# The first k-tile behind three post-norms split into an old-X part and a normalised part

## Chip, cores and metric

One core of one Trainium2 chip. The metric is the device time of the whole kernel in microseconds (us), the median of several runs; lower is better.

## What is computed

Two transformer blocks over a sequence of 512 with model width 1024, all in f32. The first has a mixer (convolution and eight-head forgetting attention), a memory cross attention and a squared-ReLU MLP; each of these three is wrapped in an RMS norm before and an RMS norm behind:

```python
for l in range(DEPTH):
    h = rms_norm(x, norm_mix_pre[l])
    y = hybrid_mixer(h, ...)
    x = x + rms_norm(y, norm_mix_post[l])
    h = rms_norm(x, norm_mem_pre[l])
    y = memory_cross_attention(h, mem_n, ...)
    x = x + rms_norm(y, norm_mem_post[l])
    h = rms_norm(x, norm_mlp_pre[l])
    y = squared_relu_mlp(h, w_up[l], w_down[l])
    x = x + rms_norm(y, norm_mlp_post[l])
```

The second block (differential attention with a pooling mixer, an MLP, gated linear attention, an MLP) has only norms ahead. The change touches the three places where `x = x + rms_norm(y, post)` is followed by a norm and a projection of the new x: into the memory queries, into the MLP and into the second block's queries.

## The kernel before

Everything is transposed: a tensor of width 1024 is eight tiles of 128 partitions by 512 tokens, so `X[:, t, :]` is tile t of the residual stream. Every weight matrix comes as 292 units of 128 x 1024 f32 values, which SyncE loads in a fixed order into four slots of `RAW`. GpSimd splits each unit into a high part `WH` (rounded to fp32r, line 278) and a low part `WL` (the rest, line 283) as soon as the unit that held the slot is used up (semaphore `unit_done`). An activation is split too, into `AH` (ScalarE) and `AL` (VectorE), and each product is three matmuls: WH x AH, WH x AL, WL x AH. The order on each engine is the order of the code; semaphores join the engines.

A projection that follows a norm starts with a **quad** (`quad`, lines 387 to 419): four output tiles in PSUM banks 0 to 3 are built together, one k-tile (one input tile) after the other, 12 matmuls of 128x512 each, so that TensorE can start as soon as the first input tile is there. A norm's row scale is applied to the output (`RB`), so the quad works on x times the gain, not on the normalised x.

In front of three of these quads stands a **post-norm**:

- `y_out` (ScalarE, lines 1327 to 1335) squares each tile of y and stores y times its gain in `Y`; VectorE sums the squares in `y_sum`; TensorE forms the column sum in bank 7 with two products by a matrix of ones (`post_stat`, lines 451 to 455), and ScalarE makes 1/sqrt of it in bank 7 (lines 1105 and 1107). After the MLP the same is done with `post=True`.
- `x_update` (VectorE, lines 1898 to 1920): for each tile, `scaled(t)` writes Y x bank 7 into a bank (line 1903), the next instruction adds that to X (line 1913), and `low` makes `AL` from X and `AH` (line 1593). `add_square` adds the squares of the new x (line 1907), for the next norm's statistic.
- `normed_post` (ScalarE): for each tile of the new X the high part `AH` (line 1120) and the square (line 1123).

In the quad behind it k-tile 0 runs its eight products with `AH` first (lines 398 and 399) and then four with `AL` (line 402); k-tiles 1 to 7 wait for `AL` (lines 413 to 415). The three post-norms are called o1 (its quad m2, the memory queries), o2 (quad m3, the MLP's first four tiles) and m3 (quad b, the second block's queries).

## Time and profile before

| | us |
|---|---|
| runs | 1835.21, 1834.85, 1832.19 |
| median of the runs | 1834.85 |
| the profiled execution, first to last instruction (span) | 1833.2 |
| TensorE busy in it | 1778.5 (97%) |
| VectorE busy | 1039.9 (57%) |
| GpSimd busy | 1055.2 (58%) |
| ScalarE busy | 452.9 (25%) |

The profile gives for the profiled execution its span alone; what lies around the span is not in it. A timeline row has the start in us, the duration, the engine, the line of the code, the operation, what it writes and reads, and in square brackets how long the engine had been idle and who ended that. PE is TensorE, PEld its weight load, DVE is VectorE, ACT ScalarE, POOL GpSimd. A matmul of 128x512 is shown with 0.39 us, but the next one starts 0.23 us after it, since they overlap; starts are the thing to compare.

### The profile page before, as it was taken

What the parts mean: (1) busy time and instruction counts of PE and PEld (TensorE: products, weight loads), DVE (VectorE), ACT (ScalarE), POOL (GpSimd) and SP (SyncE); (2) the same over time, 40 slices, a digit from 0 to 9 for tenths busy, and PEclk for the clock granted to TensorE, in tenths of its full rate; (3) what the DMA queues carried; (4) which work ended last, traced back from release to release, by engine and by line L of the source; (5) the groups of instructions that cost most, each with busy time, mean ns of one, the idle gap of its engine ahead of it and who ended that gap; (6) DMA issues with size and microseconds to landing.
All of it is one profiled execution on the core that took longest, in us unless ns stands there. A gap on an engine that the chain in (4) does not pass through costs nothing.

```text
span 1833.2 us, 22531 instructions
## 1 busy us (share of the span) xinstructions
PE 1778.5 (97%) x8318; PEld 1444.7 (79%) x8318; DVE 1039.9 (57%) x1209; ACT 452.9 (25%) x915; POOL 1055.2 (58%) x590
## 2 busy tenths in 40 slices
PE   8998899999999998999999999999999999999998
PEld 7875677788888886767888888887888888888886
DVE  4989546754343576175635252696766562626177
ACT  5215435411010123153201010212345320102011
POOL 7562462566666665533666666675344566666672
PEclk9999999999999999999999999999999999999999
DMA  6231121233333232311332333322122233333331
GB/s 238 81 97 42 47 91 47 80 92 102 94 94 101 92 102 93 92 47 47 93 102 92 104 92 98 97 92 82 56 70 60 78 98 98 93 103 92 101 94 46
DMA packets 46589, 161.42 MB, mean 88 GB/s; under 512 B 5232, under 2 KB 7792, under 8 KB 46384
## 3 DMA queue, kind: packets, MB, share of 16 engines
q1 hardware_dynamic: 45088, 157.31, 27.9%
q10 hardware_dynamic: 1424, 3.01, 0.5%
q8 instruction: 57, 0.93, 0.2%
q14 instruction: 20, 0.16, 0.0%
HBM read 158.20 MB, written 2.10 MB: 87 GB/s over the span
## 4 chain that ended last, share of the span: by engine, by line
PE 91%; DVE 6%; ACT 2%; issue 1%; DMA 0%; POOL 0%; DVEq 0%; ACTq 0%
PE bank L365 21%; PE bank L366 21%; PE bank L367 21%; PE bank L413 3%; PE bank L414 3%; PE bank L415 3%; DVE bank L1698 2%; PE bank L984 1%; PE bank L954 1%; PE bank L956 1%; PE bank L955 1%; PE bank L999 1%; PE bank L1001 1%; PE bank L1000 1%; PE bank L491 1%
## 5 line engine op out<-in xcount | busy, mean ns | idle before, releaser
L283 POOL TENSOR_TENSOR WL<-RAW,WH 128x1024 fp32r<-128x1024 f32 x291 | 739.3, 2541 | 24.3
L278 POOL TENSOR_SCALAR WH<-RAW 128x1024 fp32r<-128x1024 f32 x291 | 312.5, 1074 | 720.8 <-PE bank L367 380.0
L365 PE MATMUL bank<-AH,WH 128*128 128x512 f32 x848 | 332.2, 392 | 0.0
L367 PE MATMUL bank<-AH,WL 128*128 128x512 f32 x848 | 330.0, 389 | 0.0
L366 PE MATMUL bank<-AL,WH 128*128 128x512 f32 x848 | 330.0, 389 | 0.0
L365 PE MATMUL bank<-HH,WH 128*128 128x512 f32 x832 | 325.2, 391 | 0.0
L367 PE MATMUL bank<-HH,WL 128*128 128x512 f32 x832 | 323.9, 389 | 0.0
L366 PE MATMUL bank<-HL,WH 128*128 128x512 f32 x832 | 323.7, 389 | 0.0
L1357 ACT ACTIVATE TMP<-bank 128x512 f32<-128x512 f32 x96 | 57.2, 596 | 776.9 <-PE bank L367 739.1
L1970 DVE TENSOR_TENSOR HL<-TMP,HH 128x512 fp32r<-128x512 f32 x96 | 238.6, 2486 | 4.0 <-ACT HH L1362 0.8
L1976 DVE TENSOR_TENSOR Y<-Y,bank 128x512 f32<-128x512 f32 x72 | 49.5, 688 | 309.2 <-PE bank L367 309.2
L1966 DVE TENSOR_TENSOR TMP<-TMP 128x512 f32<-128x512 f32 x96 | 112.7, 1174 | 175.2 <-ACT TMP L1357 175.2
L365 PEld LDWEIGHTS bank<-AH,WH 128*128 128x128 f32 x848 | 159.2, 188 | 34.9 <-issue 2.0
L366 PEld LDWEIGHTS bank<-AL,WH 128*128 128x128 f32 x848 | 159.2, 188 | 34.0 <-issue 1.2
L367 PEld LDWEIGHTS bank<-AH,WL 128*128 128x128 f32 x848 | 159.2, 188 | 33.2
L365 PEld LDWEIGHTS bank<-HH,WH 128*128 128x128 f32 x832 | 156.2, 188 | 35.7 <-DVE HL L1970 3.6
L367 PEld LDWEIGHTS bank<-HH,WL 128*128 128x128 f32 x832 | 156.2, 188 | 32.7
L366 PEld LDWEIGHTS bank<-HL,WH 128*128 128x128 f32 x832 | 156.2, 188 | 32.1
L413 PE MATMUL bank<-AH,WH 128*128 128x512 f32 x208 | 81.6, 392 | 0.0
L414 PE MATMUL bank<-AL,WH 128*128 128x512 f32 x208 | 81.0, 389 | 0.0
L415 PE MATMUL bank<-AH,WL 128*128 128x512 f32 x208 | 80.9, 389 | 0.0
L1698 DVE SCALAR_TENSOR_TENSOR bank<-Y,VC,bank 128x512 f32<-128x512 f32 x116 | 78.7, 754 | 0.1
(382 smaller groups left out, 2349.4 us busy)
## 6 DMA issues: line engine op xcount, KB each, us to landing
RAW<-wstream SPq DMA_DIRECT2D x291, 512.0 KB, 3.5
out<-Y SPq DMA_DIRECT2D x8, 256.0 KB, 2.3
X<-xT SPq DMA_DIRECT2D x3, 512.0 KB, 8.1
TMP<-memT ACTq DMA_DIRECT2D x1, 1024.0 KB, 8.3
MIX<-bands ACTq DMA_DIRECT2D x1, 768.0 KB, 4.9
RAW<-wstream SPq DMA_DIRECT2D x2, 256.0 KB, 3.8
X<-xT SPq DMA_DIRECT2D x2, 256.0 KB, 4.4
BF<-masks ACTq DMA_DIRECT2D x1, 352.0 KB, 4.0
```

Source lines behind the costliest of these rows:

```text
L278: nc.gpsimd.tensor_scalar(WH[:, s, :, :].rearrange("p k n -> p (k n)"), RAW[:, s, :], 1.0, 1.0, ALU.mult, ALU.mult).then_inc(sem("w_high"), 1)
L283: nc.gpsimd.tensor_tensor(WL[:, s, :, :].rearrange("p k n -> p (k n)"), RAW[:, s, :], f32(WH[:, s, :, :].rearrange("p k n -> p (k n)")), A ...
L365: mm(bank, WH[:, slot, k, :], h(k), start=(k == 0), stop=False)
L366: mm(bank, WH[:, slot, k, :], l(k), start=False, stop=False)
L367: last = mm(bank, WL[:, slot, k, :], h(k), start=False, stop=(k == KT - 1))
L413: mm(banks[j][:], wh, h(k), start=(k == 0), stop=False)
L414: mm(banks[j][:], wh, l(k), start=False, stop=False)
L415: last = mm(banks[j][:], wl, h(k), start=False, stop=(k == KT - 1))
L1357: nc.scalar.activation(TMP[:, j % 4, :], B[banks[j] if first else j % 4][:], ACT.Relu).then_inc(sem(f"{p}_relu"), 1)
L1698: ins = v.scalar_tensor_tensor(out=SG[:, cc, :] if j == CONV_W - 1 else acc, in0=U[:, cc, j:j + S], scalar=w, in1=acc, op0=ALU.mult, op1=A ...
L1966: v.tensor_tensor(TMP[:, 4 + j % 2, :], TMP[:, j % 4, :], TMP[:, j % 4, :], ALU.mult).then_inc(sem(f"{p}_hsq"), 1)
L1970: v.tensor_tensor(HL[:, j, :], TMP[:, 4 + j % 2, :], f32(HH[:, j, :]), ALU.subtract).then_inc(sem(f"{p}_hlow"), 1)
```

## The change

The first k-tile of the quad is x_new = x_old + norm(y). The old x is there before the statistic, so its product is taken first, as a product of its own:

- `x_high` (ScalarE) and `x_low` (VectorE) split old `X[:, 0, :]` times the gain into `AH[:, 7, :]` and `AL[:, 7, :]`, places that tile 7 takes over later. They stand ahead of `y_out` and `y_sum`, and for the MLP ahead of the last down projection's read-outs.
- On TensorE `post_stat` and `quad` become `post_quad`: 12 matmuls of the old x (`x_part`, lines 470 to 472) stand behind the second ones-product (behind m3 half of them stand ahead of it), then the high products of k-tiles 0 and 1 (16), then their low products (8), then k-tiles 2 to 7 as before. `unit_done` for the first unit is signalled after k-tile 1's low products.
- VectorE rounds the normalised part itself: line 1990 writes Y x gain x bank 7 into `AH[:, 0, :]`, line 1997 the same without gain into `TMP`, and line 1999 the low part of their difference. The tiles are updated in the order 1, 2, 0, 3, ..., 7.
- In the update's loop `add_square` moves from ahead of `scaled` and `low` to behind them.
- In m3 and b later products read tile 0 of the full x as well, so ScalarE and VectorE make its high and low part once more at the end (`low(q, 0, gain)`), and the first unit behind the quad takes k-tile 0 last (`first_tile_last`).

The diff's core; the calls of `x_high`, `x_low` and `post_quad` in the places named above are left out:

```diff
+POST_ORDER = (1, 2, 0, 3, 4, 5, 6, 7)
...
+            def post_quad(p, q, n, done, bank_free=None, ahead=0, last_k=None):
+                def x_part(j):
+                    if bank_free:
+                        pe.wait_ge(sem(f"{p}_yg"), nth(f"{p}_yg", bank_free[j]))
+                    wh, wl = weights(0, j)
+                    mm(B[j][:], wh, AH[:, 7, :], start=True, stop=False)
+                    mm(B[j][:], wl, AH[:, 7, :], start=False, stop=False)
+                    return mm(B[j][:], wh, AL[:, 7, :], start=False, stop=False)
+
                 pe.wait_ge(sem(f"{p}_ysum"), nth(f"{p}_ysum", 7))
                 mm(B[7][:], ONES[:], SUM, start=True, stop=False)
+                pe.wait_ge(sem("raw_split0"), nth("raw_split0", n // 4 + 1))
+                pe.wait_ge(sem(f"{q}_xh"), nth(f"{q}_xh", 1))
+                pe.wait_ge(sem(f"{q}_xl"), nth(f"{q}_xl", 1))
+                for j in range(ahead):
+                    x_part(j)
                 pe.wait_ge(sem(f"{p}_ysq"), nth(f"{p}_ysq", 8))
                 mm(B[7][:], ONES[:], TMP[:, 5, :], start=False, stop=True).then_inc(sem(f"{p}_ystat"), 1)
+                for j in range(ahead, 4):
+                    last = x_part(j)
+                last.then_inc(sem(f"{q}_xpart"), 1)
+                for k in range(2):
+                    if k == 0:
+                        pe.wait_ge(sem(f"{q}_yh"), nth(f"{q}_yh", 1))
+                    else:
+                        pe.wait_ge(sem(f"{q}_ah"), nth(f"{q}_ah", 1))
+                    for j in range(4):
+                        wh, wl = weights(k, j)
+                        mm(B[j][:], wh, AH[:, k, :], start=False, stop=False)
+                        mm(B[j][:], wl, AH[:, k, :], start=False, stop=False)
+                for k in range(2):
+                    pe.wait_ge(sem(f"{q}_al"), nth(f"{q}_al", k + 1))
+                    for j in range(4):
+                        wh, wl = weights(k, j)
+                        last = mm(B[j][:], wh, AL[:, k, :], start=False, stop=False)
+                last.then_inc(sem("unit_done"), 1)
+                for k in range(2, KT):
+                    u = k // 2
+                    if k % 2 == 0:
+                        pe.wait_ge(sem(f"raw_split{u}"), nth(f"raw_split{u}", n // 4 + 1))
+                    pe.wait_ge(sem(f"{q}_al"), nth(f"{q}_al", k + 1))
+                    for j in range(4):
+                        if last_k and k == KT - 1 and j == 2:
+                            last_k()
+                        wh, wl = weights(k, j)
+                        mm(B[j][:], wh, AH[:, k, :], start=False, stop=False)
+                        mm(B[j][:], wh, AL[:, k, :], start=False, stop=False)
+                        last = mm(B[j][:], wl, AH[:, k, :], start=False, stop=(k == KT - 1))
+                        if k == KT - 1 and j < 3:
+                            last.then_inc(sem(done), 1)
+                    if k % 2 == 1:
+                        last.then_inc(sem("unit_done"), 1)
...
+                for n, t in enumerate(POST_ORDER):
+                    x_ready(n)
+                    if t == KT - 1:
+                        act.wait_ge(sem(f"{p}_xpart"), nth(f"{p}_xpart", 1))
+                    if t:
+                        nc.scalar.activation(AH[:, t, :], X[:, t, :], ACT.Copy, scale=vec(gain, t)).then_inc(sem(f"{p}_ah"), 1)
+                    if n >= 3:
+                        act.wait_ge(sem(f"{p}_sum"), nth(f"{p}_sum", n - 2))
+                    nc.scalar.activation(B[POST_SQ[p][n % 2]][:] if n else SUM, X[:, t, :], ACT.Square).then_inc(sem(f"{p}_xsq"), 1)
+                if p != "m2":
+                    act.wait_ge(sem("unit_done"), nth("unit_done", U0[{"m3": "mlp", "b": "bq"}[p]] + 1))
+                    nc.scalar.activation(AH[:, 0, :], X[:, 0, :], ACT.Copy, scale=vec(gain, 0)).then_inc(sem(f"{p}_ah"), 1)
+
+            def x_high(q, gain):
+                nc.scalar.activation(AH[:, 7, :], X[:, 0, :], ACT.Copy, scale=vec(gain, 0)).then_inc(sem(f"{q}_xh"), 1)
...
+                first = TMP[:, 0, :]
                 dve.wait_ge(sem(f"{p}y_rb"), nth(f"{p}y_rb", 1))
-                n = scaled(0)
-                for t in range(KT):
+                done(v.scalar_tensor_tensor(out=AH[:, 0, :], in0=Y[:, 0, :], scalar=vec(gain, 0), in1=B[7][:],
+                                            op0=ALU.mult, op1=ALU.mult).then_inc(sem(f"{q}_yh"), 1), f"{q}_yh")
+                n = scaled(POST_ORDER[0])
+                for i, t in enumerate(POST_ORDER):
                     dve.wait_ge(sem("dve_step"), nth("dve_step", n))
-                    done(v.tensor_tensor(X[:, t, :], X[:, t, :], o, ALU.add).then_inc(sem(f"{p}_x"), 1), f"{p}_x")
-                    if t >= 2:
-                        add_square(t - 1)
-                    if t < KT - 1:
-                        dve.wait_ge(sem(f"{p}_x"), nth(f"{p}_x", t + 1))
-                        n = scaled(t + 1)
-                    low(q, t, gain)
+                    done(v.tensor_tensor(X[:, t, :], X[:, t, :], o if t else first, ALU.add).then_inc(sem(f"{p}_x"), 1), f"{p}_x")
+                    if i == 0:
+                        own(v.tensor_tensor(first, Y[:, 0, :], B[7][:], ALU.mult).then_inc(sem("dve_step"), 1), "dve_step")
+                        dve.wait_ge(sem(f"{q}_yh"), nth(f"{q}_yh", 1))
+                        done(v.scalar_tensor_tensor(out=AL[:, 0, :], in0=first, scalar=vec(gain, 0), in1=f32(AH[:, 0, :]),
+                                                    op0=ALU.mult, op1=ALU.subtract).then_inc(sem(f"{q}_al"), 1), f"{q}_al")
+                    dve.wait_ge(sem(f"{p}_x"), nth(f"{p}_x", i + 1))
+                    if i < KT - 1 and POST_ORDER[i + 1]:
+                        n = scaled(POST_ORDER[i + 1])
+                    if t:
+                        low(q, t, gain)
+                    if i >= 2:
+                        add_square(i - 1)
                 add_square(KT - 1)
-
+                if q != "m2":
+                    low(q, 0, gain)
```

How the instructions stand. First VectorE at the start of the update of o1 (in the rows bank7 holds 1/sqrt, bank4 is the scratch bank of `scaled`; L1593 and L1672 are `low`). Before:

```order
L1903 TENSOR_TENSOR bank4<-Y,bank7 128x512 [waits rb,ysum]
L1913 TENSOR_TENSOR X<-X,bank4 128x512 [waits dve_step]
L1903 TENSOR_TENSOR bank4<-Y,bank7 128x512 [waits x]
L1593 SCALAR_TENSOR_TENSOR AL<-X,VC,AH 128x512 [waits ah]
L1913 TENSOR_TENSOR X<-X,bank4 128x512 [waits dve_step]
L1903 TENSOR_TENSOR bank4<-Y,bank7 128x512 [waits x]
```

And now:

```order
L1990 SCALAR_TENSOR_TENSOR AH<-Y,VC,bank7 128x512 [waits rb,ysum]
L1982 TENSOR_TENSOR bank4<-Y,bank7 128x512
L1995 TENSOR_TENSOR X<-X,bank4 128x512 [waits dve_step]
L1997 TENSOR_TENSOR TMP<-Y,bank7 128x512
L1999 SCALAR_TENSOR_TENSOR AL<-TMP,VC,AH 128x512 [waits yh,dve_step]
L1982 TENSOR_TENSOR bank4<-Y,bank7 128x512 [waits x]
L1672 SCALAR_TENSOR_TENSOR AL<-X,VC,AH 128x512 [waits ah]
L1995 TENSOR_TENSOR X<-X,bank4 128x512 [waits dve_step]
L1672 SCALAR_TENSOR_TENSOR AL<-X,VC,AH 128x512 [waits ah,x]
L1995 TENSOR_TENSOR X<-X,TMP 128x512 [waits dve_step]
```

Three instructions (L1990, L1997, L1999) stand around the first tile where there were two, and the first add to X has one of them ahead of it.

Then the same engine further on, one tile of the loop; L1907 and L1986 are `add_square`. Before:

```order
L1907 TENSOR_TENSOR TMP<-TMP,bank6 128x512 [waits xsq]
L1903 TENSOR_TENSOR bank4<-Y,bank7 128x512 [waits x,sum]
L1593 SCALAR_TENSOR_TENSOR AL<-X,VC,AH 128x512 [waits ah]
L1913 TENSOR_TENSOR X<-X,bank4 128x512 [waits dve_step]
L1907 TENSOR_TENSOR TMP<-TMP,bank5 128x512 [waits xsq]
```

And now:

```order
L1986 TENSOR_TENSOR TMP<-TMP,bank6 128x512 [waits xsq]
L1995 TENSOR_TENSOR X<-X,bank4 128x512 [waits dve_step,sum]
L1982 TENSOR_TENSOR bank4<-Y,bank7 128x512 [waits x]
L1672 SCALAR_TENSOR_TENSOR AL<-X,VC,AH 128x512 [waits ah]
L1986 TENSOR_TENSOR TMP<-TMP,bank5 128x512 [waits xsq]
```

The add to X (L1913, now L1995) is followed by the product and the low part, and the sum of squares is behind them instead of between.

Last TensorE from the second ones-product on, before:

```order
L455 MATMUL bank7<-TMP,ONES 128x512 [waits ysq]
L398 MATMUL bank0<-AH,WH 128x512 [waits ah,raw_split0]
L399 MATMUL bank0<-AH,WL 128x512
L398 MATMUL bank1<-AH,WH 128x512
L399 MATMUL bank1<-AH,WL 128x512
L398 MATMUL bank2<-AH,WH 128x512
L399 MATMUL bank2<-AH,WL 128x512
L398 MATMUL bank3<-AH,WH 128x512
L399 MATMUL bank3<-AH,WL 128x512
L402 MATMUL bank0<-AL,WH 128x512 [waits al]
L402 MATMUL bank1<-AL,WH 128x512
```

And now, from the last of the old x's products (L470 to L472) on:

```order
L470 MATMUL bank3<-AH,WH 128x512 [waits yg]
L471 MATMUL bank3<-AH,WL 128x512
L472 MATMUL bank3<-AL,WH 128x512
L493 MATMUL bank0<-AH,WH 128x512 [waits yh]
L494 MATMUL bank0<-AH,WL 128x512
L493 MATMUL bank1<-AH,WH 128x512
L494 MATMUL bank1<-AH,WL 128x512
L493 MATMUL bank2<-AH,WH 128x512
L494 MATMUL bank2<-AH,WL 128x512
L493 MATMUL bank3<-AH,WH 128x512
L494 MATMUL bank3<-AH,WL 128x512
L493 MATMUL bank0<-AH,WH 128x512 [waits ah]
```

The high products now wait for `yh`, VectorE's L1990, and those of k-tile 1 follow them ahead of any low product.

## Rows read from the trace of the kernel before

**Rows 1.** The page, section 1: engine, busy us, share of the span, instructions.
```profile
PE 1778.5 (97%) x8318; PEld 1444.7 (79%) x8318; DVE 1039.9 (57%) x1209; ACT 452.9 (25%) x915; POOL 1055.2 (58%) x590
```

**Rows 2.** Waits of PE: line <- releaser: us in total, times, longest.
```profile
PE bank L398 <- ACT AH L1120: 11.2, 3, 3.7
```

**Rows 3.** Timeline, first post-norm: start, us, engine, line [idle before <- releaser].
```profile
258.83 1.11 PE L455 MATMUL bank<-TMP,ONES 128*128 128x512 f32 x2
...
261.36 0.70 DVE L1903 TENSOR_TENSOR bank<-Y,bank 128x512 f32<-128x512 f32 x1 [6.89 <-ACT bank L1107]
262.09 0.69 DVE L1913 TENSOR_TENSOR X<-X,bank 128x512 f32<-128x512 f32 x1
262.81 0.72 ACT L1120 ACTIVATE AH<-X,VC 128x512 fp32r<-128x512 f32 x1 [1.55 <-DVE X L1913]
263.57 0.75 DVE L1593 SCALAR_TENSOR_TENSOR AL<-X,VC,AH 128x512 fp32r<-128x512 f32 x1
263.68 0.47 PE L398 MATMUL bank<-AH,WH 128*128 128x512 f32 x1 [3.73 <-ACT AH L1120]
```

**Rows 4.** Timeline of DVE, same quad, one tile of the update.
```profile
270.26 0.69 DVE L1903 TENSOR_TENSOR bank<-Y,bank 128x512 f32<-128x512 f32 x1
270.87 0.74 DVE L1593 SCALAR_TENSOR_TENSOR AL<-X,VC,AH 128x512 fp32r<-128x512 f32 x1
271.53 0.68 DVE L1913 TENSOR_TENSOR X<-X,bank 128x512 f32<-128x512 f32 x1
272.13 0.68 DVE L1907 TENSOR_TENSOR TMP<-TMP,bank 128x512 f32<-128x512 f32 x1
272.84 0.69 DVE L1903 TENSOR_TENSOR bank<-Y,bank 128x512 f32<-128x512 f32 x1
```

**Rows 5.** Timeline of POOL and DVE, same quad, later tiles.
```profile
271.17 1.36 POOL L278 TENSOR_SCALAR WH<-RAW 128x1024 fp32r<-128x1024 f32 x1 [9.38 <-PE bank L415]
272.61 2.40 POOL L283 TENSOR_TENSOR WL<-RAW,WH 128x1024 fp32r<-128x1024 f32 x1
273.45 2.10 DVE L1593 SCALAR_TENSOR_TENSOR AL<-X,VC,AH 128x512 fp32r<-128x512 f32 x1
...
282.05 1.05 POOL L278 TENSOR_SCALAR WH<-RAW 128x1024 fp32r<-128x1024 f32 x1 [1.59 <-PE bank L415]
282.48 1.16 DVE L1593 SCALAR_TENSOR_TENSOR AL<-X,VC,AH 128x512 fp32r<-128x512 f32 x1 [0.27 <-ACT AH L1120]
```

**Rows 6.** Timeline of PE, same quad: first matmuls of k-tiles 1 and 7.
```profile
268.09 0.40 PE L413 MATMUL bank<-AH,WH 128*128 128x512 f32 x1
...
284.42 0.39 PE L413 MATMUL bank<-AH,WH 128*128 128x512 f32 x1
```

**Rows 7.** Windows: us, PE, PEld, DVE, ACT, POOL busy, PEclk, DMA share, GB/s.
```profile
190.00:192.00 2.00, 1.56 (x6) 1.39 (x7) 2.00 (x6) 0.90 (x4) 0.07 (x1) 0.50 0.37 66
202.00:204.00 2.00, 1.21 (x6) 1.07 (x7) 2.00 (x5) 0.87 (x4) 0.56 (x1) 1.00 0.24 31
264.60:268.00 3.40, 3.40 (x10) 2.70 (x9) 3.27 (x6) 2.12 (x4) 0.00 (x0) 0.51 0.06 24
```

**Rows 8.** Timeline of PE in the first attention: two waits.
```profile
190.44 0.87 PE L613 MATMUL bank<-IDENT,Y 128*128 128x128 f32 x3 [2.54 <-DVE Y L1872]
...
202.79 0.30 PE L613 MATMUL bank<-IDENT,Y 128*128 128x128 f32 x1 [1.25 <-DVE Y L1872]
```

**Rows 9.** Timeline, second and third post-norm: first DVE product, k-tile 7.
```profile
337.37 0.70 DVE L1903 TENSOR_TENSOR bank<-Y,bank 128x512 f32<-128x512 f32 x1 [4.09 <-ACT bank L1107]
...
360.44 0.39 PE L413 MATMUL bank<-AH,WH 128*128 128x512 f32 x1
...
696.17 0.70 DVE L1903 TENSOR_TENSOR bank<-Y,bank 128x512 f32<-128x512 f32 x1 [3.22 <-ACT bank L1107]
...
719.10 0.39 PE L413 MATMUL bank<-AH,WH 128*128 128x512 f32 x1
```

**Rows 10.** Timeline of DVE, first MLP chunk, its last up tile.
```profile
386.66 1.11 DVE L1966 TENSOR_TENSOR TMP<-TMP 128x512 f32<-128x512 f32 x1 [1.52 <-ACT TMP L1357]
```

60 lines of the change are left out of this document (37 added, 23 removed).

## Prediction

> **What bounds the kernel now.** I read the page first: TensorE is busy for 97% of the span [rows 1], so a change pays only where TensorE waits, or where it runs slowly. The list of TensorE's waits comes second: it waits three times for ScalarE's first high part behind a post-norm, 11.2 us in all, 3.7 us each [rows 2]. Third the timeline of one of the three: the second ones-product is over at 258.83 + 1.11 = 259.94, VectorE's first product starts at 261.36, and between that and the first matmul at 263.68 lie a product, an add and the rounding [rows 3]. Fourth the clock: from 264.60 to 268.00 the granted clock is 0.51, half speed, so those 3.40 us do the work of 1.73 [rows 7]. The visible prize is thus about 3.7 + 1.67 = 5.4 us at each of three places.
>
> The view that decides comes fifth: VectorE in the rest of the quad. Call the start of its first product R (261.36). The last low part, tile 7's, ends at 282.48 + 1.16 = 283.64, or R + 22.28; TensorE starts k-tile 7 at 284.42, R + 23.06 [rows 5, 6]. So **TensorE is only 0.78 us behind VectorE** at the end. Whatever is won in front, the quad can't end more than about 0.6 us sooner unless VectorE's chain from R to tile 7 gets shorter. And it is this chain that the change lengthens.
>
> **The change part by part.** I follow both engines in us after R, to the start of k-tile 7; behind that nothing but the tile's own matmuls and the next statistic is left, as before.
>
> R itself stays. The extra splits of the old x (one ScalarE and one VectorE instruction in each place) fall where VectorE idles: it had waited 6.89 us before R at o1, 4.09 at o2 and 3.22 at m3 [rows 3, 9]; if that cover were gone, each would cost some 0.75 us, one low part's length.
>
> TensorE in front: 12 matmuls of the old x from 259.94, R - 1.42. Its pace is (284.42 - 268.09) / 72 = 0.227 us a matmul [rows 6], so they end at R + 1.30. The high products of k-tiles 0 and 1 (8 each) and the low ones (4 each) have their inputs at about 0.9, 3.0, 3.6 and 4.9; they end near 6.6. Before, k-tile 1 ended at 268.09 + 2.72, R + 9.45: the front gains some 2.8 us. They don't reach the end.
>
> VectorE: the steps between starts are read from rows 4: 0.60 behind an add that the next instruction needs nothing of, 0.71 behind an `add_square` (the engine waits for it), 0.61 behind a product, 0.66 behind a low part; and 0.73 from a product to the add that reads it, 0.72 from an add to what reads it, 0.76 from the start of a rounding on ScalarE to the low part [rows 3]. With the order that now stands in the code: L1990 at 0 (taken as a low part, the only two-input instruction of its kind in the rows; 0.69 as a product), product 1 at 0.66, add 1 at 1.39, L1997 at 1.99, L1999 at 2.72, product 2 at 3.38, low 1 at 3.99, add 2 at 4.65, low 2 at 4.65 + 0.72 + 0.76 = 6.13, add 0 at 6.79, product 3 at 7.51, add_square at 8.12, add 3 at 8.83, low 3 at 10.31.
>
> Two things make this dearer than before. One is **the new order of the loop**. Before, a tile took 0.60 + 0.71 + 0.61 + 0.66 = 2.58 us, under TensorE's 12 x 0.227 = 2.72, because the sum of squares ran while ScalarE rounded. Now the low part waits for the rounding (1.48 after the add) and the sum comes after: 1.48 + 0.66 + 0.71 = **2.85 us a tile**, over 2.72. From here on VectorE sets the pace.
>
> The other is **GpSimd**. When it splits a weight unit, a low part that starts meanwhile doesn't end until 0.54 us after GpSimd's instruction: 273.45, 2.10 long, ends at 275.55 against 275.01; 282.48, 1.16 long, ends at 283.64 against 283.10 (its rounding from 282.05, 1.05 long) [rows 5]. The product at 272.84, which reads bank 7 in PSUM, takes its usual 0.69 beside the same subtraction [rows 4]. Before, this cost 1.35 us once and the slack of 0.14 us a tile won some back. Now its phase is tied to the k-tiles: GpSimd starts when an odd k-tile ends, 3.08 us after that tile's start (282.05 against 268.09 + 4 x 2.72), takes 1.05 for WH and, 0.08 later, 2.40 for WL [rows 5]. So WL runs from 4.21 to 6.61 after the start a of k-tile 3 or 5. The low part two tiles on starts at a - 0.15 - 0.75 + 2 x 2.85 = a + 4.80, always inside WL; it ends at 6.61 + 0.54 = 7.15, and with 0.15 from the end of a rounding to TensorE's start (263.53 to 263.68 [rows 3]) the next odd k-tile starts at **a + 7.30 instead of a + 5.44**.
>
> For k-tile 3: k-tile 1's last matmul starts at 6.38, GpSimd at 6.96. It takes 1.36 as at 271.17, where a low part ran at its start as add 0 now does, then 0.08, then 2.40: until 10.80. Low 3, started at 10.31, ends at 11.34; k-tile 3 starts at 11.49. Then k-tile 5 at 18.79 and **k-tile 7 at 26.09**. Before they stood at 23.06 (o1), 360.44 - 337.37 = 23.07 (o2) and 719.10 - 696.17 = 22.93 (m3) [rows 6, 9]. The change costs 3.03 + 3.02 + 3.16 = **9.2 us**.
>
> A page of the Trainium skill, SBUF — State Buffer, section Who interferes with whom, goes further than these rows: of a VectorE instruction with two SBUF inputs and a GpSimd instruction that reads SBUF, whichever issues first holds the shared ports and the other blocks. It thereby names add 0 too, the only add to X whose second operand is not in PSUM; the rival "add 0 comes second" below takes it up from the rows.
>
> What goes at nothing: the second making of tile 0's parts (m3 and b, 0.75 us on VectorE, 0.72 on ScalarE) falls beside four units of TensorE; with it VectorE starts its MLP work some 2 us later relative to TensorE, and it had 1.52 us of idle before the last up tile, after working off its backlog [rows 10]. If that cover fails, it is 0.5 to 2 us once. The waits added for `xh`, `xl` and the bank reads end before the ones-product they stand at. If the old x's products came late, TensorE would still wait for VectorE later, so that alone would change nothing.
>
> The sum: 1833.2 + 9.2 = 1842.4 us of span. The profiled execution lies 1.65 under the median of the runs (1834.85), as span without what is around it; the same added to the median gives **1844.0 us**. A measurement of this kernel can tell about 0.2%, 3.7 us, from no change.
>
> **The rivals.**
>
> - *VectorE sets the pace, but GpSimd misses it* (0.13). If the low parts 3, 5 and 7 fell between GpSimd's instructions, low 3 would end at 11.06 and low 7 four periods later at 22.46; k-tile 7 at 22.61, that is 0.45, 0.46 and 0.32 sooner: 1833.6 us, no change. For it speaks that 0.7 us of phase decides; against it, that WL's window reaches 0.59 us ahead of the low part's start and 1.8 behind it.
> - *One of the two later low parts is held* (0.10): 1.60 less at each place, about 4.4 us over before: 1839.2.
> - *Add 0 comes second* (0.09). It starts 0.17 us before GpSimd's rounding in my sum. If GpSimd is first, until 6.96 + 1.05 = 8.01, add 0 ends at 8.55 as a low part would, instead of 7.47: the chain slips 1.08, low 3 ends at 12.14, free, 0.80 later than above; three times, 1846.4.
> - *The clock falls in the new waits* (0.10). TensorE would now stand still for about 1.7 us before k-tiles 3, 5 and 7. In the rows a wait of 1.25 us left the clock at 1.00, one of 2.54 us was followed by 0.50 [rows 7, 8]; 1.7 lies between. A fall at k-tiles 3 or 5 is taken up by the waits behind; at k-tile 7 it costs 1.67 us as it does now, at most 5.0 in all: 1849. The Trainium skill, TensorE: Matmul & The Clock Gate, section What's actually happening, says that the throttled clock is the default and recent activity releases it, which is the same danger; whether 1.7 us is enough no row here shows.
> - *Faster, on TensorE's own pace* (0.04). If VectorE kept ahead, 84 matmuls from 1.30 put k-tile 7 at 20.35: 2.7, 2.7 and 2.6 sooner, 1826.8. It would need low 7 by 20.2, 2.1 us before it ends now, though the chain has one more instruction. The point that decides is whether low 3 ends before R + 10.
>
> **How the numbers follow.** The forecast has 0.54 and its own width is about 1841 to 1846.5 (0.8 us a place, either way). With the rivals above it, slower by over 0.2% gets 0.54 + 0.10 + 0.09 + 0.10 - 0.06 for a mix of small misses = 0.77; within 0.2% 0.16, the first rival and some misses; faster 0.07. The range of 1837 to 1849 leaves out the first and the last rival.
>
> **What would show it.** Right: TensorE has no wait of 3.7 us behind the ones-product, the clock stays at 1.00 there, and new waits for `AL` of about 1.8, 1.7 and 1.7 us stand before k-tiles 3, 5 and 7; low 5 and low 7 take about 2.3 us and end 0.54 us after a GpSimd subtraction; VectorE is without idle time except before each low part; k-tile 7 starts at R + 26. Wrong: a distance from R to k-tile 7 of 23 or less, a low part that runs in 0.75 us while GpSimd subtracts, or new waits outside these three quads.

## Result and profile after

| | before | changed |
|---|---|---|
| runs, us | 1835.21, 1834.85, 1833.08, 1832.19 | 1843.44, 1842.96, 1842.29, 1841.11 |
| median | 1833.96 | 1842.62 |
| profiled execution: time, span | 1834.85, 1833.2 | 1842.29, 1840.5 |

The ratio is 1.0047 with a 95% interval of 1.0034 to 1.0060: the change makes the kernel some 8.7 us slower. A second set, c1 below, gives the same ratio. All spans, waits and distances below are of profiled executions.

The page of the changed kernel, busy times (before: [rows 1]), and in the list of waits three of TensorE's groups:

```profile
PE 1786.4 (97%) x8354; PEld 1446.9 (79%) x8354; DVE 1047.7 (57%) x1217; ACT 453.9 (25%) x917; POOL 1054.1 (57%) x590
```

```profile
PE bank L510 <- DVE AL L1672: 13.4, 12, 1.4
...
PE bank L700 <- DVE TMP L1886: 2.3, 1, 2.3
...
PE bank L493 <- DVE AH L1990: 0.8, 1, 0.8
```

The three waits of 3.7 us for ScalarE's high part [rows 2] are gone. In their place stand 12 waits for low parts, nine of them of 1.4 us: before k-tiles 3, 5 and 7 of each quad. The 0.8 us for `yh` (L1990) is at m3 alone, where half of the old x's products stand ahead of the gap. "Low 3" is the low part of tile 3, "low 5" that of tile 5, and so on. The timeline of TensorE at the first post-norm, only rows with idle time ahead of them:

```profile
264.26 0.47 PE L510 MATMUL bank<-AH,WH 128*128 128x512 f32 x1 [0.25 <-DVE AL L1672]
268.72 0.50 PE L510 MATMUL bank<-AH,WH 128*128 128x512 f32 x1 [1.45 <-DVE AL L1672]
276.04 0.50 PE L510 MATMUL bank<-AH,WH 128*128 128x512 f32 x1 [1.40 <-DVE AL L1672]
283.37 0.50 PE L510 MATMUL bank<-AH,WH 128*128 128x512 f32 x1 [1.37 <-DVE AL L1672]
```

VectorE in the same quad: R, then low 3, one whole tile (269.30 to 272.16) and the held low 5 and low 7. GpSimd's splits of those stretches stand below them.

```profile
257.19 0.75 DVE L1990 SCALAR_TENSOR_TENSOR AH<-Y,VC,bank 128x512 fp32r<-128x512 f32 x1 [6.96 <-ACT bank L1167]
...
267.55 1.11 DVE L1672 SCALAR_TENSOR_TENSOR AL<-X,VC,AH 128x512 fp32r<-128x512 f32 x1
...
269.30 0.69 DVE L1995 TENSOR_TENSOR X<-X,bank 128x512 f32<-128x512 f32 x1
270.02 0.70 DVE L1982 TENSOR_TENSOR bank<-Y,bank 128x512 f32<-128x512 f32 x1
270.77 0.75 DVE L1672 SCALAR_TENSOR_TENSOR AL<-X,VC,AH 128x512 fp32r<-128x512 f32 x1
271.44 0.68 DVE L1986 TENSOR_TENSOR TMP<-TMP,bank 128x512 f32<-128x512 f32 x1
272.16 0.69 DVE L1995 TENSOR_TENSOR X<-X,bank 128x512 f32<-128x512 f32 x1
...
273.64 2.35 DVE L1672 SCALAR_TENSOR_TENSOR AL<-X,VC,AH 128x512 fp32r<-128x512 f32 x1
...
281.03 2.28 DVE L1672 SCALAR_TENSOR_TENSOR AL<-X,VC,AH 128x512 fp32r<-128x512 f32 x1 [0.86 <-ACT AH L1183]
```

```profile
271.92 1.06 POOL L281 TENSOR_SCALAR WH<-RAW 128x1024 fp32r<-128x1024 f32 x1 [3.80 <-PE bank L512]
273.06 2.38 POOL L286 TENSOR_TENSOR WL<-RAW,WH 128x1024 fp32r<-128x1024 f32 x1
279.25 1.05 POOL L281 TENSOR_SCALAR WH<-RAW 128x1024 fp32r<-128x1024 f32 x1 [3.81 <-PE bank L512]
280.38 2.39 POOL L286 TENSOR_TENSOR WL<-RAW,WH 128x1024 fp32r<-128x1024 f32 x1
```

A tile takes 272.16 - 269.30 = 2.86 us where it took 2.58 [rows 4]. The subtraction of 273.06 is over at 275.44, low 5 at 275.99; that of 280.38 at 282.77, low 7 at 283.31, and TensorE starts k-tile 7 at 283.37, R + 26.18. At o2 it is R + 26.17, at m3 R + 26.19. Before it was 23.06, 23.07, 22.93 [rows 6, 9]. The three quads lose 3.12 + 3.10 + 3.26 = **9.48 us**.

The span grew by 7.3 us. Distances between the three R's (before [rows 3, 9]; now 257.19, 336.58, 698.64) give the account: +3.38, +3.26 and, from m3's R to its k-tile 7, +3.26; behind that +1.55; ahead of the first R 4.17 less. No edit stands in either of the last two stretches. The +1.55 lies at a wait in the second block that both kernels have (2.45 us). In the windows behind it (the last three numbers are the granted clock, the DMA share and GB/s) the clock is 0.83 over 10 us in the kernel before and 0.66 now, so about 3.4 us at half speed there and 6.8 here, 1.7 us of work:

```profile
1290.00:1300.00 10.00, 9.38 (x51) 8.42 (x51) 7.38 (x18) 3.90 (x11) 0.00 (x0) 0.83 0.02 6
```

```profile
1296.00:1306.00 10.00, 9.52 (x41) 8.51 (x42) 6.50 (x16) 3.02 (x8) 0.00 (x0) 0.66 0.01 6
```

The 4.17 us ahead of R come in three parts. The first 1.4 are there from the start: TensorE's first matmuls stand 0.43 us apart, and it goes over to 0.23 at about 12.1 us in the kernel before and at 9.2 us in the changed one. The next 1.3 come at a wait in the first mixer, which is 2.3 us long now (above), and in the kernel before

```profile
PE bank L639 <- DVE TMP L1807: 5.1, 1, 5.1
```

The last 1.5 come in the attention behind it, where the granted clock is 0.50 for 6.8 us from 158.9 and from 189.6 in the kernel before, and for 3.4 us from 159.4 and from 186.7 now.

The mixer's wait is the quads' mechanism once more. VectorE makes two instructions with two inputs in SBUF there while GpSimd splits a unit. In the kernel before GpSimd starts 0.10 us ahead, and the second of them ends 0.54 us after the subtraction:

```profile
156.56 2.00 DVE L1806 TENSOR_TENSOR Y<-MIX 128x1024 f32<-128x1024 f32 x1
158.60 2.71 DVE L1807 TENSOR_TENSOR TMP<-Y 128x512 f32<-128x512 f32 x1
```

```profile
156.46 1.04 POOL L278 TENSOR_SCALAR WH<-RAW 128x1024 fp32r<-128x1024 f32 x1 [4.81 <-PE bank L549]
157.58 3.19 POOL L283 TENSOR_TENSOR WL<-RAW,WH 128x1024 fp32r<-128x1024 f32 x1
```

In the changed kernel's profile VectorE starts 0.58 us ahead, and the pair ends 2.7 us sooner:

```profile
155.98 1.23 DVE L1885 TENSOR_TENSOR Y<-MIX 128x1024 f32<-128x1024 f32 x1
157.24 1.41 DVE L1886 TENSOR_TENSOR TMP<-Y 128x512 f32<-128x512 f32 x1
```

```profile
156.56 1.55 POOL L281 TENSOR_SCALAR WH<-RAW 128x1024 fp32r<-128x1024 f32 x1 [4.84 <-PE bank L610]
158.19 2.67 POOL L286 TENSOR_TENSOR WL<-RAW,WH 128x1024 fp32r<-128x1024 f32 x1
```

### The profile page after: what moved, and what is told of

Its sections match the earlier page's. It is cut to its first block, busy times and chain, and to the rows that moved or that the text cites. A ratio compares the mean times of both kernels' runs of the same rounds, so it can differ in the third digit from the quotient of the medians.

```text
span 1840.5 us, 22629 instructions
## 1 busy us (share of the span) xinstructions
PE 1786.4 (97%) x8354; PEld 1446.9 (79%) x8354; DVE 1047.7 (57%) x1217; ACT 453.9 (25%) x917; POOL 1054.1 (57%) x590
## 4 chain that ended last, share of the span: by engine, by line
PE 87%; DVE 8%; ACT 2%; issue 2%; DMA 0%; POOL 0%; DVEq 0%; ACTq 0%
PE bank L368 21%; PE bank L369 21%; PE bank L370 21%; PE bank L425 2%; PE bank L423 2%; PE bank L424 2%; DVE bank L1777 2%; PE bank L1044 1%; PE bank L1014 1%; DVE X L1995 1%; PE bank L1016 1%; PE bank L1015 1%; ACT AH L1183 1%; DVE AL L1672 1%; PE bank L1061 1%
## 5 line engine op out<-in xcount | busy, mean ns | idle before, releaser
L368 PE MATMUL bank<-AH,WH 128*128 128x512 f32 x848 | 332.2, 392 | 0.0
L370 PE MATMUL bank<-AH,WL 128*128 128x512 f32 x848 | 330.0, 389 | 0.0
L369 PE MATMUL bank<-AL,WH 128*128 128x512 f32 x848 | 330.0, 389 | 0.0
L1435 ACT ACTIVATE HH<-TMP 128x512 fp32r<-128x512 f32 x96 | 61.1, 637 | 3.0
L1672 DVE SCALAR_TENSOR_TENSOR AL<-X,VC,AH 128x512 fp32r<-128x512 f32 x47 | 55.4, 1179 | 6.3 <-ACT AH L1183 5.2
L423 PE MATMUL bank<-AH,WH 128*128 128x512 f32 x124 | 48.2, 389 | 0.0
```

Source lines behind the costliest of these rows:

```text
L368: mm(bank, WH[:, slot, k, :], h(k), start=(i == 0), stop=False)
L369: mm(bank, WH[:, slot, k, :], l(k), start=False, stop=False)
L370: last = mm(bank, WL[:, slot, k, :], h(k), start=False, stop=(i == KT - 1))
L423: mm(banks[j][:], wh, h(k), start=(k == 0), stop=False)
L1435: nc.scalar.activation(HH[:, j, :], TMP[:, j % 4, :], ACT.Square).then_inc(sem(f"{p}_hhigh"), 1)
L1672: done(v.scalar_tensor_tensor(out=AL[:, t, :], in0=X[:, t, :], scalar=vec(gain, t), in1=f32(AH[:, t, :]), op0=ALU.mult, op1=ALU.subtract). ...
```

## The experiments

Theory A is the prediction's: VectorE's chain from R, with the low parts that GpSimd's subtraction holds, sets the start of k-tile 7. "K7" is that start after R, at o1, o2 and m3, from one profile of each run; it was 23.06, 23.07, 22.93 in the kernel before and 26.18, 26.17, 26.19 in the changed one. Ratios are to runs of the kernel before that were taken together with each run.

| run | median us | ratio to before (95%) | K7 |
|---|---|---|---|
| changed, again (c1) | 1842.80 | 1.0047 (1.0033 to 1.0060) | 26.20, 26.16, 26.18 |
| e1 old loop | 1838.29 | 1.0025 (1.0016 to 1.0035) | 24.54, 24.52, 24.52 |
| e2 old x late | 1844.35 | 1.0059 (1.0045 to 1.0073) | 26.36, 26.06, 26.06 |
| e3 splits late | 1840.99 | 1.0035 (1.0022 to 1.0049) | 23.04, 23.03, 23.05 |
| e4 before, filler | 1839.80 | 1.0028 (1.0016 to 1.0040) | 25.42, 25.37, 25.41 |
| e5 changed, halves | 1829.34 | 0.9966 (0.9952 to 0.9980) | 24.14, 24.14, 24.20 |
| e6 before, halves | 1824.56 | 0.9944 (0.9931 to 0.9958) | 22.80, 24.07, 23.74 |
| e7 new order, halves | 1825.64 | 0.9953 (0.9940 to 0.9967) | 23.16, 23.16, 23.14 |
| e8 before, halves, filler | 1826.07 | 0.9954 (0.9941 to 0.9968) | 23.25, 23.23, 23.21 |
| e9 before, quarters | 1823.43 | 0.9941 (0.9928 to 0.9955) | 22.83, 24.02, 23.74 |
| e10 new order, quarters | 1819.42 | 0.9924 (0.9910 to 0.9937) | 22.21, 22.23, 22.20 |
| e11 changed, quarters | 1822.35 | 0.9938 (0.9924 to 0.9951) | 23.37, 23.36, 22.76 |

**e1: the old loop.** In the changed kernel:

```diff
+                    if i >= 2:
+                        add_square(i - 1)
                     dve.wait_ge(sem(f"{p}_x"), nth(f"{p}_x", i + 1))
...
-                    if i >= 2:
-                        add_square(i - 1)
```

> The change, with one thing undone: in the update's loop add_square(i - 1) stands again ahead of the next product and the low part, as before; the result is the same. Theory A (VectorE's chain, with its phase to GpSimd's subtraction, sets the start of k-tile 7): a tile takes 2.58 us instead of 2.85, k-tile 7 starts 24.2 us after R (26.1 to 26.2 in the changed kernel, 23.06 before), some 1.9 us sooner at each of three places: about 1837 us. The low part of tile 7 is then no longer held (0.75 us long); for low 5 hundredths of a microsecond decide, and if it dodges too, k-tile 7 stands at 22.4 and the time near 1832. Rival B (the cost is the extra instructions that the first tile needs on VectorE, whatever the loop): nothing is won beyond measurement, 1842. Rival C (TensorE's own pace and its waits in front set the end): no change either, and k-tile 7 stays at R + 26.

Measured 1838.29 (1837 expected), K7 24.5 (24.2 expected). About half of the change's cost is the one moved instruction. Low 7 is free, low 5 not; it lost by 0.01 us. VectorE and GpSimd at o2:

```profile
350.77 2.91 DVE L1672 SCALAR_TENSOR_TENSOR AL<-X,VC,AH 128x512 fp32r<-128x512 f32 x1
...
357.74 0.79 DVE L1672 SCALAR_TENSOR_TENSOR AL<-X,VC,AH 128x512 fp32r<-128x512 f32 x1 [0.29 <-ACT AH L1183]
```

```profile
350.76 2.36 POOL L286 TENSOR_TENSOR WL<-RAW,WH 128x1024 fp32r<-128x1024 f32 x1
...
358.07 2.71 POOL L286 TENSOR_TENSOR WL<-RAW,WH 128x1024 fp32r<-128x1024 f32 x1
```

Low 7 started 0.33 us ahead of the subtraction, took its usual time, and the subtraction was the longer. Rivals B and C fall.

**e2: nothing in the gap.** In `post_quad` the wait for `yh` moves ahead of all twelve products of the old x:

```diff
-                for j in range(ahead):
-                    x_part(j)
...
-                for j in range(ahead, 4):
+                pe.wait_ge(sem(f"{q}_yh"), nth(f"{q}_yh", 1))
+                for j in range(4):
                     last = x_part(j)
```

> The change, with the old x's product taken out of the gap: its 12 matmuls stand behind the wait for line 1990's result, so that TensorE idles in the gap again and nothing is won in front; VectorE's and ScalarE's orders stay; the result is the same. Theory A: the front never reached the end, and a later k-tile 1 starts GpSimd's split later, so that the later low parts meet the subtraction in another phase: k-tile 7 at R + 24.4 to 24.5, some 1.6 us sooner at each place, about 1838 us, faster than the changed kernel although its purpose is taken away, with the granted clock at 0.5 behind the ones-product again. Rival C (what the front wins reaches the end): each place loses the 1.42 us of products in the gap and up to 1.7 us of clock, 4 to 9 us in all: 1847 to 1852. Rival D (GpSimd has no part in it, VectorE alone sets the end): no change, 1842.6.

Measured 1844.35: a miss of theory A's number, and of rival C's. TensorE stands idle for 2.2 us in each gap. Behind it the clock was at 0.5 again at o2 and m3, but not at o1, where it stayed at 1.00. K7 hardly moved: 26.06 at o2 and m3, 0.1 us *sooner* with an empty gap, and 26.36 at o1, 0.2 later. What fills the gap is worth nothing at the end. I had taken low 7 as free; it was held in another phase. VectorE's and GpSimd's rows at o2:

```profile
353.25 1.91 DVE L1671 SCALAR_TENSOR_TENSOR AL<-X,VC,AH 128x512 fp32r<-128x512 f32 x1
...
363.16 2.86 DVE L1671 SCALAR_TENSOR_TENSOR AL<-X,VC,AH 128x512 fp32r<-128x512 f32 x1 [0.86 <-ACT AH L1182]
```

```profile
352.22 2.39 POOL L286 TENSOR_TENSOR WL<-RAW,WH 128x1024 fp32r<-128x1024 f32 x1
...
363.10 2.37 POOL L286 TENSOR_TENSOR WL<-RAW,WH 128x1024 fp32r<-128x1024 f32 x1
```

0.06 us decided. The 1.6 us that the median stands over the changed kernel do not come from here: from the first R to the end e2 took 1842.5 - 260.47 = 1582.0 us, the changed kernel 1583.3; ahead of R it had the mixer's wait of 5.1 us instead of 2.3.

**e3: the splits behind VectorE's chain.** `unit_done` for the quad's units 1 and 2:

```diff
-                        mm(B[j][:], wh, AH[:, k, :], start=False, stop=False)
+                        high = mm(B[j][:], wh, AH[:, k, :], start=False, stop=False)
+                        if k == KT - 1 and j < 2:
+                            high.then_inc(sem("unit_done"), 1)
...
-                    if k % 2 == 1:
+                    if k == KT - 1:
```

> The change, with the end of the quad's second and third unit signalled late: not when k-tiles 3 and 5 end, but by the first two high products of k-tile 7's banks 0 and 1, so that GpSimd's splits of the next units fall behind VectorE's chain and not beside it; TensorE's, VectorE's and ScalarE's orders stay, and the result is the same. (GpSimd then overwrites no weight that is still read: slots 1 and 2 are done by then.) Theory A: low 5 and low 7 take 0.75 us, k-tile 7 starts at R + 22.9 (26.1 to 26.2 now), 3.2 us sooner at each place: about 1833, which is the kernel before. Low 3 is still held, by the split that k-tile 1 releases. Rival D (VectorE's chain is longer by its own instructions and orders, and the held low parts only look so): no gain, 1842; the 2.3 us of low 5 and low 7 then come from something else and stay. Rival E: the later splits make the weight units behind the quad late, and what is won comes back as waits for raw_split of 1 to 3 us behind the quad: 1838 to 1842.

In the quads it did what theory A said: low 5 and low 7 take 0.75 us, K7 is 23.0, 3.1 us sooner. That is the direct proof that the hold was GpSimd's, and rival D falls. The time shows only 1.6 us of the 9.4 (1840.99 measured, 1833 expected). Rival E had the right size and the wrong wait. Behind o1 the late splits meet the softmax, and its `TENSOR_SCALAR`, 0.35 us long in the changed kernel, is held too, the first time beside GpSimd's rounding (288.44 to 289.49), the second beside its subtraction (289.57 to 291.92):

```profile
288.47 1.16 DVE L1721 TENSOR_SCALAR TMP<-TMP,SUMI 128x256 f32<-128x256 f32 x1
...
290.07 2.00 DVE L1721 TENSOR_SCALAR TMP<-TMP,SUMI 128x256 f32<-128x256 f32 x1
```

TensorE waits there for 1.63 and 1.17 us, and the granted clock is 0.50 from 290.0 to about 296.8:

```profile
290.00:292.00 2.00, 0.95 (x4) 0.24 (x2) 1.96 (x3) 0.83 (x3) 1.92 (x1) 0.51 0.60 223
```

Behind o2 VectorE's backlog into the MLP has no idle time left [rows 10], and TensorE waits 1.55, 0.37 and 0.36 us for it at 391.95 to 394.61. Only m3's gain stays: from its R to the end 1139.0 us against 1141.9.

**e4: the clock alone.** In the kernel before, behind the second ones-product:

```diff
+                pe.wait_ge(sem("raw_split0"), nth("raw_split0", n // 4 + 1))
+                for j in range(4):
+                    if free:
+                        pe.wait_ge(sem(f"{p}_yg"), nth(f"{p}_yg", free[j]))
+                    for _ in range(3):
+                        mm(B[j][:], WH[:, 0, j, :], HH[:, 0, :], start=True, stop=True)
```

> The kernel before, with 12 filler matmuls of 128x512 behind the second ones-product of each of the three post-norms, into banks 0 to 3, where the quad's first products then overwrite them (start=True): the output is the same, and the 2.7 us of work fill the gap with nothing useful, so that only the clock in front of the quad is changed; VectorE, ScalarE and GpSimd keep their instructions and orders. Theory A (TensorE is 0.8 us behind VectorE at the end, and an earlier k-tile 1 moves GpSimd's phase onto the low parts): the clock stays at 1.00, the first two k-tiles run 1.7 us sooner, and yet k-tile 7 comes at R + 25.1 instead of 23.06, 2.0 us later at each place: about 1840 us. Rival C (the clock's loss behind the gap is a loss of the end): 1.67 us sooner at each place, 1829. Rival F (VectorE's slack of 0.8 us is all that can be won): up to 0.6 us sooner at each, 1832.

Measured 1839.80; K7 25.4 (25.1 expected). The clock stays at 1.00, VectorE's program is the old one, and the kernel is 5.6 us slower, because k-tile 1 ends earlier and GpSimd's split now begins 0.02 us ahead of low 3 (348.08) and level with low 5 (355.39), at o2:

```profile
348.08 2.90 DVE L1599 SCALAR_TENSOR_TENSOR AL<-X,VC,AH 128x512 fp32r<-128x512 f32 x1
...
355.39 2.91 DVE L1599 SCALAR_TENSOR_TENSOR AL<-X,VC,AH 128x512 fp32r<-128x512 f32 x1
```

```profile
348.06 2.37 POOL L283 TENSOR_TENSOR WL<-RAW,WH 128x1024 fp32r<-128x1024 f32 x1
...
355.39 2.37 POOL L283 TENSOR_TENSOR WL<-RAW,WH 128x1024 fp32r<-128x1024 f32 x1
```

So speed in front of the quad was not just worth nothing here, it cost.

**c1: the changed kernel again.**

> The changed kernel once more, unchanged, on another set of runs and with a second profile. Three of the six profiles so far reach R of the first post-norm at 257.2 to 257.8 us (a wait of 2.3 us in the first mixer), three at 260.2 to 261.4 (a wait of 5.1 us at the same place), and the kernel e2, which differs from the changed one only behind that place, is among the late ones. Theory: this is a difference from run to run and not the change's; the three distances from R to k-tile 7 stay at 26.2 to 26.3 whichever it is, and the median stays between 1841 and 1844. Rival: the change itself brings R forward by some 4 us; then R stands at 257.2 again.

1842.80, and 26.20, 26.16, 26.18: the three quads repeat to some hundredths. R of o1 stood at 257.59, with the short wait in the mixer, so c1 by itself doesn't separate theory and rival. The other profiles do: e2, e7 and e10, built on the changed kernel, have the long wait, and e6 and e9, built on the kernel before, the short one. All fourteen profiles sort by who starts first there. Where GpSimd is 0.1 us ahead the wait is 5.1 us with the subtraction whole (before, e2, e4), 4.0 with halves (e7, e8) and 3.5 with quarters (e10); where VectorE is 0.6 us ahead it is 2.3 or 2.4 whatever the subtraction, since the second instruction is then held by the rounding alone (over at 158.11, the instruction at 158.65 in the rows above). What goes with this is the clock behind an earlier wait of TensorE, 2.36 us long in all fourteen and over at about 142 us. In the eight profiles with VectorE ahead the granted clock is 0.50 for 3.4 us behind it, and in the six others it stays at 1.00; GpSimd's split waits for TensorE's unit (`<-PE` in the rows above), so a slower TensorE lets it start later against VectorE. In those eight TensorE had also gone over to 0.23 us a matmul sooner at the start, at 9.2 to 10.4 us against 10.8 to 12.1. That the one leads to the other is an argument and not tested, but the difference is one between executions and not the change's.

**e5: a shorter hold.** GpSimd's subtraction in two instructions:

```diff
-                    nc.gpsimd.tensor_tensor(
-                        WL[:, s, :, :].rearrange("p k n -> p (k n)"), RAW[:, s, :],
...
+                    for h in range(2):
+                        low = nc.gpsimd.tensor_tensor(
+                            WL[:, s, 4 * h:4 * h + 4, :].rearrange("p k n -> p (k n)"), RAW[:, s, h * S:h * S + S],
...
+                    low.then_inc(sem(f"raw_split{s}"), 1)
```

> The changed kernel, with GpSimd's subtraction for WL written as two instructions of 512 columns instead of one of 1024, in every weight unit; same result, same order, and the next unit's signal still with the last one. Theory A (a low part that starts beside the subtraction is held until that instruction is over): it is now held until a half is over, at most 1.2 + 0.54 us instead of 2.4 + 0.54; low 5 and low 7 take 1 to 1.7 us instead of 2.3, k-tile 7 comes at R + 23.0 to 25.0 (26.2 now), and the time is 1834 to 1839 us. Rival G (GpSimd takes the port again for the second half before VectorE gets it, so that the hold lasts through both): low 5 and 7 stay at 2.3 us and more, and the time at 1842. Rival D (no hold by GpSimd): nothing changes either, but the low parts do not follow the ends of the halves.

Low 5 and 7 take 1.27 and 1.20 us, K7 is 24.1 to 24.2, as said: VectorE gets its turn between the halves, and rival G falls. The time, 1829.34, is well under the 1834 to 1839 expected. The quads give 6.1 us of the 13.3; the rest comes from where I hadn't looked. In the profiles it lies behind the first R (1583.3 us to the end in the changed kernel, 1570.1 in e5), and 1.7 of it is a shorter stretch of half clock in the second block (3.4 us instead of 6.8).

**e6: the same in the kernel before.**

> The same halving in the kernel before. There VectorE's slack of 0.14 us a tile takes up most of what the held low parts cost, and TensorE, whose gap and half clock in front stay, sets the end: k-tile 7 stays at R + 23.0, the quads give nothing, and the time stays within 2 us of the kernel before, 1832 to 1836. If it is faster by more than 3 us, the hold costs elsewhere too (it would be seen as shorter VectorE instructions behind the mixer and in the attention); if slower, by more than 3, GpSimd's extra instruction does it.

1824.56, 10 us faster than before. The expectation of no change was wrong, and its "if faster" branch holds. The same group in the kernel before, in e6 and in e9:

```profile
L1970 DVE TENSOR_TENSOR HL<-TMP,HH 128x512 fp32r<-128x512 f32 x96 | 238.6, 2486 | 4.0 <-ACT HH L1362 0.8
```

```profile
L1971 DVE TENSOR_TENSOR HL<-TMP,HH 128x512 fp32r<-128x512 f32 x96 | 152.6, 1590 | 4.2 <-ACT HH L1363 1.0
```

```profile
L1971 DVE TENSOR_TENSOR HL<-TMP,HH 128x512 fp32r<-128x512 f32 x96 | 106.0, 1105 | 4.5 <-ACT HH L1363 1.3
```

These 96 instructions of the MLPs were 2.49 us long on average; the shortest of them, with no split beside them, take 0.69. VectorE's busy time falls from 1039.9 to 917.6 us. From m3's R to the end the kernel wins 5.2 us, of which 2.6 are two groups of TensorE's waits for VectorE, one down from 3.0 to 1.5 and one from 2.5 to 1.4; behind the second of them the clock no longer falls to 0.50 for 3.4 us, another 1.7. Ahead of o1's R the profile is 4.6 us shorter, but that isn't all the halves' doing: in e6's profile VectorE comes first in the mixer (2.3 us of wait instead of 5.1). e8, which has the same code up to there and GpSimd first, as in the kernel before, reaches R at 258.70, 2.7 us sooner than before. How the 10 us of the medians divide between shorter holds and this order is not shown. The quads themselves win nothing: at o2 and m3 K7 is even 1.0 and 0.8 later, because the half clock behind the empty gap lasted longer there (this is o2, 6.2 to 7.2 us after R, where the kernel before is back at 1.00):

```profile
338.80:339.80 1.00, 1.00 (x4) 0.71 (x4) 0.96 (x3) 0.74 (x2) 0.00 (x0) 0.50 0.00 0
```

**e7: another order on VectorE, with halves.** The new order from R: L1990, product 1, add 1, L1997, L1999, product 2, low 1, add 2, add 0, product 3, low 2, add 3, squares 1 and 2, product 4, low 3, then a tile as in the kernel before.

> The changed kernel with the halved subtraction and another order on VectorE: the sums of squares of tiles 1 and 2 moved behind add 3, the first tile's instructions packed ahead, and from tile 4 on the old loop with add_square ahead of the product and the low part; same result. Theory A: without any hold VectorE would reach low 7's end at 20.5 to 20.6 and TensorE, on its own pace from the old x's product, k-tile 7 at R + 21.6; with holds of at most 1.2 + 0.54 us on two or three low parts, of which the loop's slack takes up 0.14 a tile, k-tile 7 comes at R + 22.0 to 23.3, up to 1 us sooner than before at each place: 1831 to 1834.5 us, the first form of the change that is not slower than the kernel before. Rival C (the end follows the front): same numbers, but then e5 would have shown no gain. Rival G (hold through both halves): k-tile 7 at 24 or later, 1836 and more.

K7 23.16, in the expected band, 1.0 us under e5. The time is 5 us under the band (1831 expected at the least), for e6's reason, and not better than e6.

**e8: filler and halves in the kernel before.**

> The kernel before with the halved subtraction (as e6, 1824.6) and with e4's 12 filler matmuls in each of the three gaps, so that the clock stays up; the output is the same. On the kernel before the filler cost 6 us, since an earlier k-tile 1 moved GpSimd's subtraction onto two low parts and each was held for 2.2 us. Theory A: with holds of at most about 1 us each, which the loop's slack of 0.14 us a tile and the 0.8 us at the end take up in part, the 1.7 us of clock in front now reach the end in part: k-tile 7 at R + 22.0 to 23.0 (about 23.7 in e6's second and third post-norm), 0.5 to 1.7 us sooner at each place: 1819.5 to 1823. Rival H (a k-tile 1 that comes early never pays, whatever the hold): 1825 to 1831, as e4 against the kernel before. Rival F (VectorE's own chain, 20.6 us and the two latencies, is the end): k-tile 7 at R + 23, 1824.

1826.07: e4's loss of 5.6 us is gone with the shorter hold. But a gain can't be shown either: K7 is 0.8 and 0.5 us sooner than in e6 at o2 and m3 and 0.4 later at o1, and the time is level within the intervals. Theory A's 1819.5 to 1823 was missed, and the time lies in rival H's band (1825 to 1831), so H isn't refuted by it. Against H stands the profile alone: with a mixer wait of 4.0 us against 2.3, e8 takes 1565.5 us from the first R to the end and e6 1566.6.

**e9 and e10: quarters.** The subtraction in four instructions of 256 columns, in the kernel before and in e7.

> The kernel before with the subtraction in four instructions of 256 columns. VectorE's instructions with two inputs in SBUF were 2.77 us long beside one of 1024 columns and 1.66 beside halves, in the MLPs; 0.69 is their length alone. Theory A: the hold lasts at most 0.6 + 0.5 us: these come down to 1.1 to 1.4 us, VectorE's busy time (1039.9 before, 917.6 with halves) to 840 to 890; but what TensorE still waits for is little (some 2.6 us of its waits in the second block went with the halves), and GpSimd's unit grows from 3.52 us to about 3.9 and with holds 4.5, under the 5.44 us of a unit on TensorE: 1821.5 to 1825.5. Rival J (GpSimd becomes the bound: four instructions, each held by VectorE in turn, pass 5.4 us a unit, and TensorE waits for WL): over 1828, with waits for raw_split in the MLPs.

> The change with e7's order on VectorE (1825.6 with halves, k-tile 7 at R + 23.0) and the subtraction in four. Theory A: low 3 and low 5, held for 1.5 and 1.8 us in e7, come down to 1.1 to 1.4; k-tile 7 at R + 21.8 to 22.5, 0.5 to 1.2 us sooner at each place: 1821.5 to 1824.5. If it stands no better than e9, the split of the first k-tile has no gain to give even where the hold is short; if it stands 1.5 to 4 us under e9, that is the change's own worth. Rival J as for e9.

Busy times of e9 and of e10:

```profile
PE 1773.5 (97%) x8318; PEld 1445.7 (79%) x8318; DVE 846.5 (46%) x1209; ACT 452.7 (25%) x915; POOL 1253.9 (69%) x1463
```

```profile
PE 1778.8 (98%) x8354; PEld 1446.1 (79%) x8354; DVE 852.7 (47%) x1217; ACT 454.4 (25%) x917; POOL 1256.2 (69%) x1463
```

e9, 1823.43, is in its band, and VectorE's busy time too. GpSimd doesn't become the bound; TensorE waits for a `WL` behind the start only once, 1.4 us (rival J). e10, 1819.42, is 2 us under its band and beats both kernels, by 14.6 us the one before. Of these 10.6 are the quarters' (e9) and 4.0 those of the change with the new order. K7 is 22.2, and TensorE's wait before k-tile 3 at o2 is down to

```profile
342.22 0.50 PE L511 MATMUL bank<-AH,WH 128*128 128x512 f32 x1 [0.61 <-DVE AL L1673]
```

**e11: the change as it stands, with quarters.**

> The change as it stands, its own order on VectorE included, with the subtraction in four instructions of 256 columns (1842.6 with one, 1829.3 with two). It tells what part of e10's 1819.4 comes from the order on VectorE and what from the shorter hold. Theory A: VectorE's loop of 2.85 us a tile is then all that is left; without any hold k-tile 7 would stand at R + 22.5, with holds of up to 1.1 us on low 3, 5 and 7 at R + 23.2 to 23.8 (24.1 with halves, 22.2 in e10): 1823 to 1827 us, 3 to 6 us over e10 and no better than the kernel before with quarters (1823.4). Rival K (the order on VectorE matters no more once the hold is short): within 1.5 us of e10, 1819 to 1821.

1822.35, just under the band. It lies 2.9 us over e10, and its three K7 are 1.2, 1.1 and 0.6 us later: VectorE's order still counts, and rival K falls. Against the kernel before with the same subtraction, the change as written stands at +8.2 us with one instruction (c1), +4.8 with two, -1.1 with four (e11 against e9, which can't be told from zero), and with the other order at -4.0 (e10 against e9).

## The prediction, step by step

It said 1844.0 (1837 to 1849), slower; measured 1842.62.

- *Old x in the gap*: done at R + 1.15 (1.30 predicted). k-tile 2 starts at R + 7.07, 2.4 us sooner than before (2.8 predicted). That this doesn't reach the end: shown by e2 and e4.
- *New loop*: 2.86 us a tile (2.85). That it costs: shown by e1, 1.64 to 1.67 us a place.
- *Held low parts*: they end 0.55 and 0.54 us after the subtraction (0.54); low 3 ends at R + 11.47 (11.34), low 5 at 18.80, low 7 at 26.12. That GpSimd is the cause: shown by e3 and e5.
- *K7*: 26.18 (26.09), and 9.48 us for the three quads (9.2). Its first 0.13 us come from GpSimd: its rounding behind k-tile 1 started at R + 7.02 (6.96) and took 1.43 (1.36), and low 3 was held the longer; low 3 itself started at 10.36 (10.31). From a low part's end to TensorE it is 0.06 us, not 0.15, which gives some of it back.
- *Waits in TensorE's rows*: 1.45, 1.40, 1.37, where I said 1.8, 1.7, 1.7. I had counted from start to start; the row counts from the modelled end of the last matmul.
- *Clock*: it stayed at 1.00 through waits of 1.4 us in every quad, so that rival was rightly a rival.
- *Add 0 second*: it started at 264.04, 0.17 us ahead of GpSimd's rounding (my sum's number), and took 0.68; the rounding took 1.43 instead of 1.05. The page SBUF — State Buffer of the Trainium skill, section Who interferes with whom, has whoever issues first keep the shared pair and the other block until it finishes; the rows of e1 and of this add agree, both ways round.
- *Low 0 once more*: hidden, no wait of TensorE between o2's quad and m3's post-norm.
- *The sum*: 1.4 us high on the median, though the quads cost 0.3 more than I said. What I had not reckoned with are the two parts outside them, 4.17 less ahead of R and 1.55 more in the second block; they belong to how an execution falls out, and a median carries some of each. The mechanism and its size in the quads were right; that the median came as near as 1.4 us is partly luck, since such parts alone are of 2 to 4 us.

What failed is not in the prediction but in expectations behind it. In e2 I gave one K7 for a case in which hundredths of a microsecond decide between held and free. In e6 I priced the hold only where TensorE's longest waits stood, and the times of e5 and e7 came out 5 us under their bands for the same reason. In e3 I gave the quads' gain to the whole kernel. In e8 I took K7's gain at o2 and m3 for a gain in time.

## To carry to other kernels

Before filling a gap of the busiest engine, follow the engine that feeds it to the last consumer of the stage: here TensorE was 0.78 us behind VectorE at the end, and any speed in front could only move a third engine's work into VectorE's way. Where GpSimd streams long instructions beside VectorE, try cutting them: here the hold of each VectorE instruction shrank with GpSimd's instruction, for 0.1 to 0.4 us more of GpSimd a unit where nothing stood in the way (2.39 us whole, 2.5 halved, 2.8 quartered), and 0.4 and 0.8 us on average over all units. And moving an engine's work behind the critical chain pays only if what stands there has slack; in e3 two of three places had none. And when two profiles differ where no edit stands, look who came first there before calling it noise: the mixer's wait was 2.3 or 5.1 us by the same race that decides the quads.
